# Even layer: input projections, sample-row scores and the index stage's loads put into one pipeline

## The chip, the cores and the metric

One NeuronCore of one Trainium2 chip runs the whole step; the metric is device time in microseconds (us). Before the change the median of three runs is 2185.47 us (2183.77 to 2185.55).

## The reference, cut to what matters

The model has two layers; the change touches the first part of layer 0 (the even layer). There are 1024 prompt rows and 8 sample rows (one new token for each of 8 sequences with 256 cached positions). All is float32.

```python
h = jnp.einsum('btd,de->bte', x, e_w_in[e])                  # 1024 + 8 rows, 1024 -> 4168 columns
q, k, v, qi, ki, wi, ga, ub, vb, gb = jnp.split(h, EVEN_SPLIT, axis=-1)
# index score of a key s for a row t, both groups; the 256 best keys are kept (64 for a sample row)
sc = jnp.einsum('bthd,bsd->bths', qi, ki) * (IDX_DIM ** -0.5)
score = jnp.einsum('bths,bth->bts', jax.nn.relu(sc), wi * (IDX_HEADS ** -0.5))
_, idx = lax.top_k(score, topk)
# attention logits: q.k / 8 - slope * distance, softmax over the kept keys; then times silu(ga)
```

q, k, v, qi, ga, ub, vb and gb are 512 columns wide each, ki is 64 and wi is 8.

## The kernel before

The program is a list of phases. Each has its own tiles and semaphores and ends in a barrier of all engines, after which the next phase issues its first load. The first three matter here.

**phase_even_in** (L105). SP loads an identity, x in row tiles of 128 (`x_tok`; the ninth tile is the 8 sample rows) and the weights of one column segment at a time into `w`, two deep. TensorE (PE) transposes x into `xT`, then runs `order`: for each segment (QI, Q, K, then KI with WI, 72 columns) nine groups, one for each row tile, of 8 accumulating matmuls (L186) into one of 8 PSUM banks. A float32 matmul shows in the trace as two instructions. VectorE (DVE) and ScalarE (ACT) take turns copying a bank to `stage` (L199), and POOL stores it to the scratch tensor `h` in DRAM (L156). The sample rows' group uses the same 512-column matmuls with 8 rows of output.

**phase_sample_scores** (L240). SP reads the sample rows of qi, wi, q and others back from `h`, two of them broadcast to all 128 partitions (L277 to L285, semaphore `own_in`), and the cached keys by page (L291, L292, `cache_in`). DVE forms the index scores (L336 to L343) and the logits (L345, L346) of the 8 sample rows. PE runs the GA segment beside it: `gate_columns` for row tiles 0 to 5, then a wait for DVE's scores and a transpose (L370), then tiles 6 and 7 and the sample rows, then the transposes of the logits (L377). The GA sample rows use `strips` (L95): four 128-column pieces of the weights go to four 32-row strips of the output. ACT makes the sigmoid and a copy, POOL multiplies them (L314), SP stores.

**phase_index** (L399). SP reads the identity, ki, qi and wi of all prompt rows back from `h` (L453 to L460, semaphore `in1`); PE waits for all eight loads, transposes ki and qi (L530), then runs 160 score matmuls (L537), each followed by a Relu on ACT and a weighted sum on DVE into `score`. Then SP's reload of q and k is transposed (L544), and PE runs the last four segments V, UB, VB, GB (L555, and L95 for the sample rows) out of `src`, loaded at L469 once the transposes are done. Meanwhile DVE searches each row's threshold, 31 rounds of seven counts (L633), and marks the kept keys (L659 to L663). The next phase, phase_attend, begins with a memset at L722.

Of the kernel before, what the change touches and what calls it, by code (L numbers as in the profile page):

```python
# [7 lines left out]
F32 = mybir.dt.float32  # L8
# [96 lines left out]
def phase_even_in(nc, g, xT):  # L105


    with ExitStack() as c:
        sb = lambda n, s, d=F32: c.enter_context(nc.sbuf_tensor(n, s, d))
        sem = phase_semaphores(nc, c, "")  # L110
        ident = sb("ei_ident", [P, P])
        x_tok = sb("ei_x", [P, NT + 1, D])
        w = sb("ei_w", [P, 2, KD, AW])
        w_small = sb("ei_ws", [P, KD, HD + H])
        stage = sb("ei_stage", [P, NB, AW])
        ps = [c.enter_context(nc.psum_tensor(f"ei_ps{i}", [P, AW], F32)) for i in range(NB)]
        ident_in, x_in = sem("ei_ident_in"), [sem(f"ei_x_in{t}") for t in range(NT + 1)]
        w_in = [sem(f"ei_w_in{i}") for i in range(2)]
        ws_in = sem("ei_ws_in")
        tr_done, xT_done = sem("ei_tr_done"), sem("ei_xT_done")  # L120
        mm_done = sem("ei_mm_done")
        ev_v, ev_a = sem("ei_ev_v"), sem("ei_ev_a")
        out_done = [sem(f"ei_out{i}") for i in range(NB)]
        W = g["e_w_in"]

        segs = [(COL_QI, AW), (COL_Q, AW), (COL_K, AW), (COL_KI, HD + H)]
        order = [(si, t) for si in range(len(segs)) for t in range(NT + 1)]
        wide = [si for si in range(len(segs)) if segs[si][1] == AW]
        h_d = g["h"]

        block = c.enter_context(nc.Block())

        @block.sync
        def _(sp):
            sp.dma_start(ident[:], g["c_ident"]).then_inc(ident_in, 16)
            for t in range(NT):
                sp.dma_start(x_tok[:, t, :], g["x_prompt"][t * P:(t + 1) * P, :]).then_inc(x_in[t], 16)
            sp.dma_start(x_tok[0:DB, NT, :], g["x_sample"]).then_inc(x_in[NT], 16)
            for n, si in enumerate(wide):
                if n >= 2:  # L140

                    sp.wait_ge(mm_done, (wide[n - 2] + 1) * (NT + 1))
                c0 = segs[si][0]
                sp.dma_start(w[:, n % 2], W[:, c0:c0 + AW].rearrange("(k p) n -> p k n", p=P)).then_inc(w_in[n % 2], 16)
                if n == 1:
                    sp.dma_start(w_small[:], W[:, COL_KI:COL_KI + HD + H].rearrange("(k p) n -> p k n", p=P)).then_inc(ws_in, 16)
            for b in range(NB):
                sp.wait_ge(out_done[b], 16 * len([n for n in range(len(order)) if n % NB == b]))

        @block.gpsimd  # L150
        def _(pool):

            for n, (si, t) in enumerate(order):
                c0, cw = segs[si]
                pool.wait_ge((ev_v, ev_a)[n % 2], n // 2 + 1)
                pool.dma_start(h_d[t * P:t * P + rows(t), c0:c0 + cw], stage[0:rows(t), n % NB, 0:cw]).then_inc(out_done[n % NB], 16)  # L156

        @block.tensor
        def _(pe):
            pe.wait_ge(ident_in, 16)  # L160
            for n in range(2 * (NT + 1)):

                t, half = n // 2, n % 2
                pe.wait_ge(x_in[t], 16)
                if n >= NB:
                    pe.wait_ge(xT_done, n - NB + 1)
                for j in range(4):
                    kd = half * 4 + j
                    m = rows(t)
                    last = nc.tensor.transpose(ps[n % NB][:, j * P:j * P + m], x_tok[0:m, t, kd * P:(kd + 1) * P], ident[0:m, 0:m])  # L170
                last.then_inc(tr_done, 1)
            pe.wait_ge(xT_done, 2 * (NT + 1))
            for n, (si, t) in enumerate(order):
                c0, cw = segs[si]
                if t == 0:
                    if cw == AW:
                        u = wide.index(si)
                        pe.wait_ge(w_in[u % 2], 16 * (u // 2 + 1))
                    else:
                        pe.wait_ge(ws_in, 16)  # L180
                if n >= NB:
                    m = n - NB
                    pe.wait_ge((ev_v, ev_a)[m % 2], m // 2 + 1)
                for kd in range(KD):
                    rhs = w[:, wide.index(si) % 2, kd, :] if cw == AW else w_small[:, kd, :]
                    last = nc.tensor.matmul(ps[n % NB][0:rows(t), 0:cw], xT[:, kd, t * P:t * P + rows(t)], rhs,  # L186
                                            start=(kd == 0), stop=(kd == KD - 1))
                last.then_inc(mm_done, 1)

        def evacuate(eng, copy, done, parity):  # L190
            for n, (si, t) in enumerate(order):
                if n % 2 != parity:
                    continue
                cw = segs[si][1]
                eng.wait_ge(mm_done, n + 1)
                if n >= NB:

                    eng.wait_ge(out_done[n % NB], 16 * (n // NB))
                copy(stage[0:rows(t), n % NB, 0:cw], ps[n % NB][0:rows(t), 0:cw]).then_inc(done, 1)  # L199

        @block.vector
        def _(dve):
            for n in range(2 * (NT + 1)):
                t, half = n // 2, n % 2
                dve.wait_ge(tr_done, n + 1)
                m = rows(t)
                nc.vector.tensor_copy(xT[:, half * 4:half * 4 + 4, t * P:t * P + m],
                                      ps[n % NB][:].rearrange("p (j n) -> p j n", j=4)[:, :, 0:m]).then_inc(xT_done, 1)
            evacuate(dve, nc.vector.tensor_copy, ev_v, 0)

        @block.scalar
        def _(act):
            evacuate(act, nc.scalar.copy, ev_a, 1)

# [21 lines left out]
def phase_sample_scores(nc, g, xT, score_s, lrow, room):  # L240
# [3 lines left out]
    with ExitStack() as c:  # L244
# [3 lines left out]
        ident = sb("sa_ident", [P, P])  # L248
        qb, qib = (r[:].rearrange("p c t -> p (c t)").rearrange("p (b n) -> p b n", b=DB) for r in room)
        w, stage, sig = sb("sa_w", [P, KD, AW]), sb("sa_stage", [P, 4, AW]), sb("sa_sig", [P, 2, AW])  # L250
        wib = sb("sa_wib", [P, DB, H])
        kc = sb("sa_kc", [P, DB, 2, AW])
        ic = sb("sa_ic", [P, DB, 2, HD])
        prod = sb("sa_prod", [P, 2, AW])
        lg = sb("sa_lg", [P, DB, 2, H])
        ix = sb("sa_ix", [P, DB, 2, H])
        sc = sb("sa_sc", [P, DB, 2])
        q_s, k_s, qi_s = sb("sa_q", [DB, AW]), sb("sa_k", [DB, AW]), sb("sa_qi", [DB, AW])
        ki_s, wi_s = sb("sa_ki", [DB, HD]), sb("sa_wi", [DB, H])
        lgn, ixn = sb("sa_lgn", [DB, H]), sb("sa_ixn", [DB, H])  # L260
        pt = sb("sa_pt", [1, 2 * DB], I32)
        ps = [c.enter_context(nc.psum_tensor(f"sa_ps{i}", [P, AW], F32)) for i in range(5)]
        ps_ga = [c.enter_context(nc.psum_tensor(f"sa_psga{i}", [P, AW], F32)) for i in range(3)]
        w_in, ga_mm, ga_read, sig_d, silu_d = (sem(f"sa_{n}") for n in ("w_in", "ga_mm", "ga_read", "sig_d", "silu_d"))
        ga_out = [sem(f"sa_ga_out{i}") for i in range(4)]
        copy_out = sem("sa_copy_out")
        own_in, cache_in, pt_in = sem("sa_own_in"), sem("sa_cache_in"), sem("sa_pt_in")
        link_v, scored, logits, tr_done, row_done = sem("sa_link"), sem("sa_scored"), sem("sa_logits"), sem("sa_tr"), sem("sa_rows")
        own_done, filled = sem("sa_own_done"), sem("sa_filled")
        block = c.enter_context(nc.Block())  # L270
        NOWN = 9

        @block.sync
        def _(sp):
            sp.dma_start(pt[:], g["page_table"]).then_inc(pt_in, 16)
            s = h_d[T:TA]
            sp.dma_start(qib, s[:, COL_QI:COL_QI + AW].partition_broadcast(P)).then_inc(own_in, 16)  # L277
            sp.dma_start(wib[:], s[:, COL_WI:COL_WI + H].partition_broadcast(P)).then_inc(own_in, 16)
            sp.dma_start(qb, s[:, COL_Q:COL_Q + AW].partition_broadcast(P)).then_inc(own_in, 16)
# [20 lines left out]
            for i in range(4):  # L300
                sp.wait_ge(ga_out[i], 16 * (len(range(i, NT, 4)) + (4 if i == NT % 4 else 0)))
# [2557 lines left out]
```

## Time and profile before

| | us |
|---|---|
| profiled execution, device time | 2195.87 |
| its span, first to last instruction | 2193.8 |
| median of three timed runs | 2185.47 |
| PE busy (share of the span) | 1832.5 (84%) |
| DVE busy | 1243.5 (57%) |
| ACT busy | 582.0 (27%) |
| POOL busy | 402.5 (18%) |

The phases run one after another, so a share of the whole span says little; each stretch has its own engine that ends last. The timeline by engine gives the start and length of merged runs of instructions and, in brackets, how long the engine was idle before and what released it. The windows view gives busy time and granted TensorE clock (1.00 is 2.4 GHz, 0.50 is 1.2 GHz) of a stretch.

### The profile page before, as it was taken

What the parts mean: (1) busy time and instruction counts of PE and PEld (TensorE: products, weight loads), DVE (VectorE), ACT (ScalarE), POOL (GpSimd) and SP (SyncE); (2) the same over time, 40 slices, a digit from 0 to 9 for tenths busy, and PEclk for the clock granted to TensorE, in tenths of its full rate; (3) what the DMA queues carried; (4) which work ended last, traced back from release to release, by engine and by line L of the source; (5) the groups of instructions that cost most, each with busy time, mean ns of one, the idle gap of its engine ahead of it and who ended that gap; (6) DMA issues with size and microseconds to landing.
All of it is one profiled execution on the core that took longest, in us unless ns stands there. A gap on an engine that the chain in (4) does not pass through costs nothing. (4 is left out here: it accounts for less than half of the span.)

```text
span 2193.8 us, 30598 instructions
## 1 busy us (share of the span) xinstructions
PE 1832.5 (84%) x11638; PEld 1061.9 (48%) x11638; DVE 1243.5 (57%) x2313; ACT 582.0 (27%) x1163; POOL 402.5 (18%) x376
## 2 busy tenths in 40 slices
PE   8999476899993899799747999977989977764977
PEld 4445234444442687447233666653454445653432
DVE  2000064888998765473467667677544244654287
ACT  0000004500012553121145555562121113432100
POOL 0001110000013554110000333320004222323030
PEclk9999688999996999797876999997989887987989
DMA  4200724212301100831175344434647275766401
GB/s 180 72 34 32 192 92 137 77 39 72 116 34 69 39 21 10 321 116 44 46 149 174 106 123 144 142 128 109 142 128 212 73 178 140 182 148 179 176 29 72
DMA packets 276431, 245.58 MB, mean 112 GB/s; under 512 B 131980, under 2 KB 229164, under 8 KB 276028
## 3 DMA queue, kind: packets, MB, share of 16 engines
q1 hardware_dynamic: 272276, 232.57, 36.0%
q0 software_dynamic: 2976, 9.02, 1.2%
q10 hardware_dynamic: 1040, 2.10, 0.4%
q8 instruction: 92, 1.51, 0.3%
q14 instruction: 47, 0.39, 0.1%
HBM read 161.53 MB, written 86.63 MB: 113 GB/s over the span
## 5 line engine op out<-in xcount | busy, mean ns | idle before, releaser
L1860 PE MATMUL ri_ps<-ri_xm,od_w 128*128 128x384 f32 (+1 forms) x768 | 233.0, 458 | 0.1
L555 PE MATMUL ix_ps<-ix_src,ei_xT 128*128 128x512 f32 x512 | 223.8, 599 | 9.4 <-DMA ix_src<-in_e_w_in 9.4
L1956 PE MATMUL ri_ps<-od_w,ri_xm 128*128 128x512 f32 x512 | 228.4, 609 | 0.0
L186 PE MATMUL ei_ps<-ei_w,ei_xT 128*128 128x512 f32 (+1 forms) x432 | 189.0, 600 | 4.0 <-DMA ei_w<-in_e_w_in 4.0
L1860 PEld LDWEIGHTS ri_ps<-ri_xm,od_w 128*128 128x128 f32 x768 | 145.1, 191 | 73.8 <-issue 2.3
L633 DVE TENSOR_SCALAR_CACHE_REDUCE ix_flags<-score,ix_cand 128x384 bf16<-128x384 f32 (+1 forms) x186 | 163.7, 942 | 12.2 <-DVE ix_cand L650 12.0
L555 PEld LDWEIGHTS ix_ps<-ix_src,ei_xT 128*128 128x128 f32 x512 | 98.0, 192 | 132.7 <-issue 123.0
L1956 PEld LDWEIGHTS ri_ps<-od_w,ri_xm 128*128 128x128 f32 x512 | 100.0, 196 | 125.5 <-issue 125.4
L1112 PE MATMUL go_psm<-go_w,go_srcT 128*128 128x512 f32 (+1 forms) x288 | 135.9, 632 | 4.5 <-DVE go_y L1254 4.2
L186 PEld LDWEIGHTS ei_ps<-ei_w,ei_xT 128*128 128x128 f32 (+1 forms) x432 | 77.8, 181 | 114.4 <-issue 114.4
L199 DVE COPY ei_stage<-ei_ps 128x512 f32<-128x512 f32 (+2 forms) x18 | 10.6, 588 | 196.5 <-PE ei_ps L186 196.5
L770 PE MATMUL at_pss<-at_kz,qT 128*128 128x512 f32 (+3 forms) x192 | 79.9, 528 | 31.5 <-POOL at_kz L722 31.5
L730 POOL TENSOR_TENSOR at_bias<-at_alibi,score 128x128 f32<-128x128 f32 (+7 forms) x64 | 91.9, 1436 | 74.9 <-ACT at_alibi L791 74.3
L1112 PEld LDWEIGHTS go_psm<-go_w,go_srcT 128*128 128x128 f32 (+1 forms) x288 | 54.9, 194 | 79.0 <-issue 76.8
L2413 PE MATMUL wk_i<-od_big 64*64 64x128 f32 (+1 forms) x1024 | 70.2, 353 | 20.6 <-DVE wk_ak L2588 8.4
L361 PE MATMUL sa_psga<-sa_w,ei_xT 128*128 128x512 f32 x128 | 60.3, 635 | 30.7 <-DMA sa_w<-in_e_w_in 30.7
L1382 PE MATMUL co_psm<-od_w,co_srcT 128*128 128x512 f32 (+1 forms) x144 | 68.4, 631 | 17.1 <-DVE co_y L1436 16.9
L840 DVE CUSTOM_DVE_ANT_0 at_s<-at_pss,at_bias 128x128 f32<-128x128 f32 (+7 forms) x64 | 48.4, 756 | 49.1 <-PE at_pss L770 48.8
L2171 DVE SCALAR_TENSOR_TENSOR ri_xm<-ri_xT,ri_mu,ri_xm 128x384 f32<-128x384 f32 (+1 forms) x144 | 70.9, 567 | 6.2 <-ACT ri_xm L1973 5.8
L760 PE MATMUL at_pso<-at_v,at_pT 128*128 128x64 f32 x576 | 73.3, 274 | 0.0
L2269 DVE TENSOR_TENSOR ri_xT<-ri_xT,ri_ps 128x512 f32<-128x512 f32 (+1 forms) x18 | 11.6, 642 | 108.1 <-ACT ri_xT L2089 108.0
L760 PEld LDWEIGHTS at_pso<-at_v,at_pT 128*128 128x128 f32 x576 | 71.9, 197 | 0.3 <-issue 0.2
(329 smaller groups left out, 3010.6 us busy)
## 6 DMA issues: line engine op xcount, KB each, us to landing
ix_src<-in_e_w_in SPq DMA_DIRECT2D x4, 2048.0 KB, 11.1
scratch_h<-ix_stage SPq DMA_DIRECT2D x32, 256.0 KB
od_w<-in_c_w_in SPq DMA_DIRECT2D x16, 512.0 KB, 5.7
od_w<-in_c_w_in SPq DMA_DIRECT2D x4, 2048.0 KB, 8.8
ei_w<-in_e_w_in SPq DMA_DIRECT2D x3, 2048.0 KB, 19.3
scratch_h<-ei_stage POOLq DMA_DIRECT2D x24, 256.0 KB, 2.3
ix_src<-scratch_h SPq DMA_DIRECT2D x3, 2048.0 KB, 9.2
go_uvg<-scratch_h SPq DMA_DIRECT2D x8, 768.0 KB, 10.5
```

The costliest lines, as they stand in the source:

```text
L186: last = nc.tensor.matmul(ps[n % NB][0:rows(t), 0:cw], xT[:, kd, t * P:t * P + rows(t)], rhs, start=(kd == 0), stop=(kd == KD - 1))
L555: last = nc.tensor.matmul(ps[n % NB][:], xT[:, kd, t * P:(t + 1) * P], w_rest[s % 2][:, kd], start=(kd == 0), stop=(kd == KD - 1))
L633: link(nc.vector.tensor_scalar(flags[:, at:at + x.shape[1]], x, s, 0.0, op, ALU.add, accum_out=cnt[:, j:j + 1]), wait=j == NTOP - 1)
L730: nc.gpsimd.tensor_tensor(bias[:, u % 2, 0:n], alibi[:, u % 2, 0:n], score[:, OFF[i]:OFF[i] + n], ALU.add).then_inc(bias_d, 1)
L760: last = nc.tensor.matmul(ps_o[i % 2][:, h * HD:(h + 1) * HD], pT[:, n % 4, j * P:(j + 1) * P], v[:, k0 + j, h * HD:(h + 1) * HD], start=( ...
L770: last = nc.tensor.matmul(ps_s[u % 2][:, s0:s0 + w], qT[:, h // 2, i * P:(i + 1) * P], kz[:, h, s0:s0 + w], start=True, stop=True)
L1112: last = nc.tensor.matmul(ps_m[k][0:m, cs], srcT[:, k, kd, 0:m], w[:, kd, cs], start=(kd == 0), stop=(kd == KD - 1))
L1382: last = nc.tensor.matmul(ps_m[k][0:m, hf * AW:(hf + 1) * AW], srcT[:, k, kd, 0:m], wo[hf][:, kd], start=(kd == 0), stop=(kd == KD - 1))
L1860: last = nc.tensor.matmul(out[:, 0:wd], w[:, ct % 2, kd, i * P:(i + 1) * P], xm[:, i, kd, lo:lo + wd], start=(kd == 0), stop=(kd == KD - 1))
L1956: last = nc.tensor.matmul(out[:], xm[:, j, kd, t * P:(t + 1) * P], w[:, a, kd], start=(kd == 0), stop=(kd == KD - 1))
L2171: nc.vector.scalar_tensor_tensor(xm[:, n % 2, kd, lo:lo + m], xT[:, kd, lo:lo + m], mu[:, MIX[n], kd:kd + 1], xm[:, n % 2, kd, lo:lo + m], ...
L2413: return nc.tensor.matmul(out, lhsT, rhs, start=start, stop=stop, skip_group_check=True)
```

## The change

phase_even_in and phase_sample_scores become one phase. Its segments are QI, KI, Q, K, GA. The sample rows of every 512-column segment use `strips`. DVE's score work for the sample rows is cut into one step for each group of Q and K. GA is gated on DVE from PSUM (ACT makes the sigmoid) and stored by POOL. At its end the phase reads qi into `w[:, 0]` and ki into a part of `x_tok`, from `h`; the identity, `w`, `x_tok` and `xT` stay allocated through phase_index, which therefore issues neither these loads nor a wait for them on PE. phase_index loads the weights of V and UB at its start into `x_tok`, and those of VB and GB into `w` after the q and k transposes; its `stage` and `sig` lie over `qiT`.

```diff
+        segs = [(COL_QI, AW), (COL_KI, HD + H), (COL_Q, AW), (COL_K, AW), (COL_GA, AW)]
+        who = ["v" if n % 2 == 0 or order[n][0] == GA else "a" for n in range(len(order))]
...
+            load_w(0)
+            sp.dma_start(w_small[:], W[:, COL_KI:COL_KI + HD + H]...).then_inc(ws_in, 16)
+            sp.dma_start(pt[:], g["page_table"]).then_inc(pt_in, 16)
+            load_w(1)
+            sp.wait_ge(pt_in, 16)
+            sp.wait_ge(tr_done, 2 * (NT + 1))
...                                    # 16 pages of ic and of kc (kc lies over x_tok)
+            load_w(2)                  # waits for QI's last matmul
+            stored_rows(small_rows[QI])
+            sp.dma_start(qib, ...partition_broadcast(P)).then_inc(index_in, 16)
+            sp.dma_start(qi_s[:], ...).then_inc(index_in, 16)
+            stored_rows(small_rows[KI])
...                                    # wib, ki_s, wi_s: index_in
+            load_w(3)                  # waits for Q's last matmul
+            stored_rows(small_rows[Q])
+            sp.dma_start(qb, ...partition_broadcast(P)).then_inc(q_in, 16)
...                                    # q_s: q_in; after K's rows are stored k_s: k_in
+            sp.wait_ge(mm_done, first[K] + NT + 1)
+            for n in range(first[QI], first[KI] + NT):
+                stored_rows(n)
+            sp.dma_start(w[:, 0], tok(COL_QI, AW)).then_inc(next_in, 16)
+            for o in range(2):
+                sp.dma_start(kid[:, :, o * HD:(o + 1) * HD], tok(COL_KI, HD)).then_inc(next_in, 16)
+            sp.wait_ge(next_in, 48)
...                                    # POOL, in its store loop:
+                if n == first[GA] + 3:
...                                    # waits for the KI and K stores, then p_k, p_idx_k, s_k, s_idx_k
...                                    # PE, in its group loop:
+                if stripped(n):
+                    last = strips(nc, ps[n % NB], lambda kd: xT[:, kd, TA - STRIP:TA], lambda kd: w[:, wide.index(si) % 2, kd])
...                                    # PE after the loop: wait scored, 2 transposes; wait logits, 16 transposes
...                                    # DVE, in its loop over the groups, after the copy of group n:
+                    if si == GA:
+                        k = n - first[GA]
+                        dve.wait_ge(sig_d, k + 1)
+                        nc.vector.tensor_tensor(stage[0:m, n % NB, 0:wd], sig[0:m, k % 2, 0:wd], src, ALU.mult).then_inc(ev["v"], 1)
...
+                if n == first[Q] + 2:
+                    own_score()        # waits index_in, ic_in
+                if first[Q] + 2 <= n < first[Q] + 2 + DB:
+                    index_score(n - first[Q] - 2)
+                if n == first[K] + 1:
+                    index_sum()
+                if first[K] + 2 <= n < first[K] + 2 + DB:
+                    logit(n - first[K] - 2)    # the first waits q_in, kc_in
+            own_logit()                # waits k_in
...                                    # phase_index
-            sp.dma_start(ident[:], g["c_ident"]).then_inc(in1, 16)
-            sp.dma_start(kid[:, :, 0:HD], tok(COL_KI, HD)).then_inc(in1, 16)
-            sp.dma_start(kid[:, :, HD:P], tok(COL_KI, HD)).then_inc(in1, 16)
-            sp.dma_start(src[0][:], tok(COL_QI, AW)).then_inc(in1, 16)
...                                    # wi, upper, bits_f, bits_i as before, then k
+            load_w(0)
+            load_w(1)
             sp.wait_ge(pe_done, n1)
+            sp.dma_start(src[0], tok(COL_Q, AW)).then_inc(in2, 16)
             sp.wait_ge(pe_done, n3)
+            load_w(2)
+            load_w(3)
...                                    # POOL
+            pool.wait_ge(pe_done, 2)
+            nc.gpsimd.memset(ones, 1.0).then_inc(ones_done, 1)
...                                    # PE
-            pe.wait_ge(in1, 16 * 8)
...                                    # DVE
-            dve.wait_ge(in1, 16 * 8)
+            dve.wait_ge(in1, 16 * 4)
```

## Rows read from the trace of the kernel before

**Rows 1.** Windows: stretch, length, busy (count) by engine, clock, DMA share, GB/s.

```profile
20.70:225.30 204.60, 204.50 (x576) 93.07 (x576) 10.59 (x18) 8.54 (x18) 19.19 (x35) 0.99 0.14 51
339.50:351.40 11.90, 0.00 (x0) 0.00 (x0) 0.00 (x0) 0.00 (x0) 2.85 (x3) 0.52 0.88 253
351.40:418.00 66.60, 65.74 (x214) 37.84 (x215) 48.46 (x81) 47.36 (x94) 0.00 (x0) 0.96 0.18 63
664.00:687.10 23.10, 0.15 (x8) 0.00 (x0) 22.35 (x22) 0.43 (x2) 1.79 (x2) 0.58 0.03 12
```

**Rows 2.** Timeline of PE to 420 us: start, length, instructions, idle before and releaser.

```profile
20.68 188.99 PE L186 MATMUL ei_ps<-ei_w,ei_xT 128*128 128x512 f32 x432 [3.98 <-DMA ei_w<-in_e_w_in]
209.59 15.61 PE L186 MATMUL ei_ps<-ei_ws,ei_xT 128*128 128x72 f32 x144
255.92 44.25 PE L361 MATMUL sa_psga<-sa_w,ei_xT 128*128 128x512 f32 x96 [30.72 <-DMA sa_w<-in_e_w_in]
314.88 0.59 PE L370 MATMUL sa_ps<-sa_ident,sa_sc 128*8 128x128 f32 x2 [14.71 <-DVE sa_sc L343]
334.77 1.91 PE L377 MATMUL sa_ps<-sa_ident,sa_lg 128*8 128x128 f32 x16 [1.57 <-DVE sa_lg L346]
351.43 7.35 PE L530 MATMUL ix_ps<-ix_ident,ix_src 128*128 128x128 f32 x40 [14.75 <-DMA ix_bits_i<-c_bits_i]
```

**Rows 3.** Timeline of PE from 420 us, the rest segments.

```profile
433.06 58.16 PE L555 MATMUL ix_ps<-ix_src,ei_xT 128*128 128x512 f32 x128 [9.44 <-DMA ix_src<-in_e_w_in]
...
493.04 55.20 PE L555 MATMUL ix_ps<-ix_src,ei_xT 128*128 128x512 f32 x128
548.17 1.95 PE L95 MATMUL ix_ps<-ix_src,ei_xT 128*32 128x128 f32 x64
550.05 55.20 PE L555 MATMUL ix_ps<-ix_src,ei_xT 128*128 128x512 f32 x128
```

**Rows 4.** Groups by line and shape, 20 to 226 us: busy, mean ns, idle before.

```profile
L186 PE MATMUL ei_ps<-ei_w,ei_xT 128*8 128x512 f32 x48 | 21.1, 592 | 0.0
```

**Rows 5.** Timeline of DVE: sample-row work, then phase_index.

```profile
269.23 0.68 DVE L323 TENSOR_TENSOR sa_q<-sa_q,sa_k 8x512 f32<-8x512 f32 x1 [44.86 <-DMA sa_ident<-c_ident]
...
293.72 1.22 DVE L339 TENSOR_REDUCE sa_ix<-sa_prod 128x16 f32<-128x1024 f32 x1
294.97 2.29 DVE L336 TENSOR_TENSOR sa_prod<-sa_ic,kT 128x1024 f32<-128x1024 f32 x1
...
361.16 0.42 DVE L610 TENSOR_SCALAR score<-ix_rel,ix_wi 128x384 f32<-128x384 f32 x1 [9.56 <-ACT ix_rel L578]
...
418.10 0.23 DVE L623 TENSOR_SCALAR score<-ix_upper 128x128 f32<-128x128 f32 x1
```

**Rows 6.** Timeline of POOL: the last stores of phase_even_in and what follows.

```profile
225.74 0.52 POOL L156 DMA_DIRECT2D scratch_h<-ei_stage  x1 [0.53 <-ACT ei_stage L199]
230.11 0.47 POOL L305 MEMSET score_s<- 128x449 f32 x1 [3.85 <-POOLq L76]
...
294.92 1.26 POOL L314 TENSOR_TENSOR sa_stage<-sa_stage,sa_sig 128x512 f32<-128x512 f32 x1 [5.96 <-ACT sa_stage L392]
...
688.09 7.50 POOL L722 MEMSET at_kz<- 64x4096 f32 x2 [22.30 <-POOLq L76]
```

**Rows 7.** Timeline of SP's queue: the read-back, and phase_index's first load.

```profile
230.41 0.37 SPq L277 DMA_DIRECT2D kT<-scratch_h  x1
...
231.45 23.23 SPq L279 DMA_DIRECT2D qT<-scratch_h  x1
...
339.52 0.37 SPq L453 DMA_DIRECT2D ix_ident<-c_ident  x1
```

**Rows 8.** Window 13 us after the copy of v to its output is issued.

```profile
565.00:570.00 5.00, 5.00 (x13) 2.19 (x12) 4.25 (x12) 0.00 (x0) 0.00 (x0) 1.00 0.21 82
```

**Rows 9.** Timeline of ACT at the end of phase_sample_scores.

```profile
333.26 0.28 ACT L389 ACTIVATE sa_sig<-sa_psga 128x128 f32<-128x128 f32 x1 [0.84 <-PE sa_psga L95]
...
336.72 2.02 ACT L395 ACTIVATE lrow<-sa_ps 8x512 f32<-8x512 f32 x4 [3.02 <-PE sa_ps L377]
```

More of the change, by code:

```diff
@@ L102, in strip_rows @@
     return slice((j + 1) * STRIP - DB, (j + 1) * STRIP)
[L105 to L213, printed above, removed]
@@ L244, in phase_sample_scores, with index_rows, phase_index @@
+def index_rows(x_tok):
+    return x_tok[:].rearrange("p t d -> p (t d)")[:, 2 * DB * AW:2 * DB * AW + T].rearrange("p (t n) -> p t n", t=NT)
+def phase_index(nc, g, xT, qT, kT, score, score_s, ident, w, x_tok):
     with ExitStack() as c:
@@ L257, in phase_sample_scores @@
[L257 to L264, printed above, removed]
@@ L352, in _ @@
-        @block.tensor
-        def _(pe):
-            def gate_columns(t):
-                if t >= 3:
-                    pe.wait_ge(ga_read, t - 2)
-                if t == NT:
-                    last = strips(nc, ps_ga[t % 3], lambda kd: xT[:, kd, TA - STRIP:TA], lambda kd: w[:, kd])
-                else:
-                    for kd in range(KD):
-                        last = nc.tensor.matmul(ps_ga[t % 3][:], xT[:, kd, t * P:(t + 1) * P], w[:, kd], start=(kd == 0), stop=(kd == KD - 1))
-                last.then_inc(ga_mm, 1)
-            pe.wait_ge(w_in, 16)
-            for t in range(NT - 2):
-                gate_columns(t)
-            pe.wait_ge(own_in, 16 * NOWN)
-            pe.wait_ge(scored, 1)
-            for pg in range(2):
-                last = nc.tensor.transpose(ps[4][0:DB, pg * P:(pg + 1) * P], sc[:, :, pg], ident[:])
-            last.then_inc(tr_done, 1)
-            for t in range(NT - 2, NT + 1):
-                gate_columns(t)
-            pe.wait_ge(logits, DB)
-            for h in range(H):
-                for pg in range(2):
-                    last = nc.tensor.transpose(ps[h // 2][0:DB, (h % 2) * PAST + pg * P:(h % 2) * PAST + (pg + 1) * P],
-                                               lg[:, :, pg, h], ident[:])
-            last.then_inc(tr_done, 1)
@@ L381, in _ @@
-        @block.scalar
-        def _(act):
-            act.dma_start(w[:], g["e_w_in"][:, COL_GA:COL_GA + AW].rearrange("(k p) n -> p k n", p=P)).then_inc(w_in, 16)
-            for t in range(NT + 1):
-                m = AW if t < NT else P
-                act.wait_ge(ga_mm, t + 1)
-                if t >= 2:
-                    act.wait_ge(silu_d, t - 1)
-                nc.scalar.activation(sig[:, t % 2, 0:m], ps_ga[t % 3][:, 0:m], ACT.Sigmoid).then_inc(sig_d, 1)
-                if t >= 4:
-                    act.wait_ge(ga_out[t % 4], 16 * (t // 4))
-                nc.scalar.copy(stage[:, t % 4, 0:m], ps_ga[t % 3][:, 0:m]).then_inc(ga_read, 1)
-            act.wait_ge(tr_done, 2)
-            for q in range(4):
-                last = nc.scalar.activation(lrow[:, 2 * q:2 * q + 2, 0:PAST],
-                                            ps[q][0:DB, :].rearrange("p (h s) -> p h s", h=2), ACT.Copy, scale=HD ** -0.5)
-            last.then_inc(row_done, 1)
@@ L400, in phase_index @@
-def phase_index(nc, g, xT, qT, kT, score, score_s):
-    with ExitStack() as c:
-        sb = lambda n, s, d=F32: c.enter_context(nc.sbuf_tensor(n, s, d))
-        sem = phase_semaphores(nc, c, "")
-        h_d = g["h"]
-        ident = sb("ix_ident", [P, P])
         wi = sb("ix_wi", [P, NT, H])
-        src = [sb(f"ix_src{i}", [P, NT, AW]) for i in range(2)]
-        kid = src[1][:, :, 0:P]
+        src, kid = [w[:, i] for i in range(2)], index_rows(x_tok)
         qiT = sb("ix_qiT", [P, 4, T])
@@ L444, in phase_index @@
         gates = [n for n, (s, t) in enumerate(rest) if is_gate[s]]
-        w_rest = src
-        w_in, rest_out = [sem(f"ix_w_in{i}") for i in range(2)], [sem(f"ix_rest_out{i}") for i in range(4)]
+        over = x_tok[:].rearrange("p t d -> p (t d)")
+        w_rest = [over[:, s * KD * AW:(s + 1) * KD * AW].rearrange("p (k n) -> p k n", k=KD) for s in range(2)] + src
+        w_in, rest_out = [sem(f"ix_w_in{i}") for i in range(4)], [sem(f"ix_rest_out{i}") for i in range(4)]
         zeroed = sem("ix_zeroed")
@@ L548, in _ @@
                 if t == 0:
[L549 removed]
+                    pe.wait_ge(w_in[s], 16)
                 bank_free()
                 if t == NT:
[L552 removed]
+                    last = strips(nc, ps[n % NB], lambda kd: xT[:, kd, TA - STRIP:TA], lambda kd: w_rest[s][:, kd])
                 else:
                     for kd in range(KD):
[L555 removed]
+                        last = nc.tensor.matmul(ps[n % NB][:], xT[:, kd, t * P:(t + 1) * P], w_rest[s][:, kd],
                                                 start=(kd == 0), stop=(kd == KD - 1))
@@ L2790, in even_layer @@
             score, qT, kT = (c2.enter_context(nc.sbuf_tensor(n, s, F32)) for n, s in (("score", [P, OFF[NT]]), ("qT", [P, 4, T]), ("kT", [P, 4, T])))
-            with nc.sbuf_tensor("ei_xT", [P, KD, TA], F32) as xT:
-                phase_even_in(nc, g, xT)
-                phase_sample_scores(nc, g, xT, score_s, lrow, (qT, kT))
-                phase_index(nc, g, xT, qT, kT, score, score_s)
+            with ExitStack() as c3:
+                xT, ident, w, x_tok = (c3.enter_context(nc.sbuf_tensor(f"ev_{n}", s, F32)) for n, s in (
+                    ("xT", [P, KD, TA]), ("ident", [P, P]), ("w", [P, 2, KD, AW]), ("x", [P, NT + 1, D])))
+                phase_even_in(nc, g, xT, score_s, lrow, (qT, kT), ident, w, x_tok)
+                phase_index(nc, g, xT, qT, kT, score, score_s, ident, w, x_tok)
             phase_attend(nc, g, qT, kT, score)
```

319 lines of the change are left out of this document (215 added, 104 removed).

## The prediction, made before the changed kernel ran

> **What bounds the kernel now.** The phases run one after another, so I read the windows first: which engine works in each stretch, and where none does [rows 1]. From 20.7 to 225.3 us PE is busy 204.5 of 204.6 us at clock 0.99: the projections are bound by PE. Behind it come stretches in which PE hardly runs; from 339.5 to 351.4 nothing runs but DMA (0.88 of its engines) and memsets of POOL. Then the timeline of PE says what ended each of PE's holes [rows 2]: the GA weights' load (30.72 us of idle time), DVE's `sa_sc` (14.71), a small wait for `sa_lg` (1.57), and the eight loads of phase_index (14.75). From 351.4 to 418.0 PE is the bound again (65.74 of 66.6). Last, DVE's timeline shows what ends phase_index [rows 5]: the threshold search starts at 418.10 with the masks, and DVE is busy 22.35 us of the last 23.1 [rows 1], up to 1 us before the next phase starts at 688.09 [rows 6]. PE's last segment ends near 664, since after it PE is busy 0.15 us of 23.1 [rows 1]. So whatever the change does to PE after 418 is not on the path; what counts is how early DVE's search starts, and that is set by PE's transposes of qi and ki at 351.43 plus 66.7 us of PE-bound work (418.10 - 351.43). The sum has to find the new time of that one instruction.
>
> **The change part by part: the joined phase.** PE starts its first matmul at 20.68 in both. The loads ahead of it (identity, x, first weights) are the same, in the same order; the second weights move behind the small ones, and 32 page loads come in only after x is transposed, all behind the first weights on SP's queue. Bounds: 4.0 us earlier (the idle time before that matmul [rows 2]) to as much later if the page loads share the engines with it; I take 0, since they are issued behind it.
>
> *QI, Q, K.* They take 209.59 - 20.68 = 188.9 us [rows 2]. The three sample-row groups are 48 of the 432 instructions [rows 4]. A segment at full clock has 128 in 55.20 us [rows 3], 0.431 each, so they cost 20.7. A group by `strips` costs 1.88 us from its start to the next segment (550.05 - 548.17), three of them 5.6. Saved: 15.1; left: 173.8.
>
> *KI* is moved, not changed: 15.6 us. *GA* costs one segment with strips as in phase_index: 550.05 - 493.04 = 57.0 us [rows 3]. It needs no wait inside if the evacuation keeps up: for each group of 6.9 us ACT makes one sigmoid (at most four times the 0.28 of 128 columns [rows 9]) and DVE one multiply out of PSUM. The latter is not in this trace; its bounds are half and all of the 1.22 us that a 128x1024 operation takes [rows 5], both far below 6.9.
>
> So PE's stream ends at 20.7 + 173.8 + 15.6 + 57.0 = 267.1 us.
>
> *DVE's work for the sample rows* is hidden beneath that stream: 32 operations of 1.22 us [rows 5] are 39 us in 116 us of Q and K. What it could cost is a wait in DVE's queue, with PSUM copies behind it. It waits at two places. At Q's third group it needs the rows of QI and KI, stored, read back and broadcast. Before, such a read-back took from 230.41 [rows 7] to 269.23 [rows 5], 38.8 us, beside a 2 MB weight load and a 2 MB copy. QI ends at 78.6 and KI at 94.2, so by that figure the last lands near 135, where DVE arrives at 115. The first bank that DVE then owes is Q's fifth group, which PE needs again eight groups on, in K's fourth, near 173. At K's second group it needs q: issued near 153, landed near 192, DVE there from 166; PE needs the bank near 224 (GA's third group). The bounds are 0 and what runs past 38 and 32 us of margin; I take 0. SP's queue is in order too: the third weights go out at 78.6 for a need at 152, the fourth at 152 for 210.
>
> *The end of the phase.* After PE's last strip: 0.59 + 1.91 us of transposes [rows 2] and ACT's last quarter of 2.02 us [rows 9], all within 3.5. The stores are later: sigmoid 0.28 [rows 9], multiply, then four stores of POOL at about 0.5, where before there was one copy and one store. Before, PE ended at 225.2 (209.59 + 15.61), the last store was issued at 225.74, and the next phase began at 230.11 [rows 6]: 4.9 us. I add 0.45 for sigmoid and multiply in place of a 0.2 us copy and 1.6 for three more stores: 7.0. The lower end is 3.5 plus the 0.8 between ACT's end (338.74 [rows 9]) and the next issue at 339.52 [rows 7]: 4.3; the upper is 7.0 plus the 4.9 us seen here once more, 12. Of the three transfers that must be done by then, the reload of qi starts after K (210.0), and p_k's copy near 238; of the same 2 MB copy of v, issued at 552.39, little is left 13 us later (DMA share 0.21 [rows 8]), so 267 covers both.
>
> The row that speaks against this end: a DVE operation on two SBUF operands started 0.05 us after a POOL operation (294.97 against 294.92) and took 2.29 in place of 1.22 [rows 5, 6]; the two engines can hold each other up. DVE now works beside all of POOL's stores, but those are eight slots of 6.9 us deep, so only the four last ones, which share their time with own_logit (operations of 0.68 us and less [rows 5]), could be late; by the rows I take 0 and keep 2 us.
> SBUF — State Buffer of the Trainium skill ("SBUF: two separate sides", the box on DVE blocking DMA) states the other side of it: POOL cannot write its DMA descriptors while DVE holds the shared port. By that rule the end comes 1 to 2 us later and the time is near 2110; no run here shows a POOL store so delayed.
>
> So phase_index begins at 267.1 + 7.0 = 274.1.
>
> **Phase_index.** PE waits for nothing and starts its transposes at 274.1, in place of 351.43: **77.3 us earlier**. Their 7.35 us stay; they follow an idle gap in both and ACT's copies pace them. DVE still waits for wi and three constants. Its first unit is due 9.7 us after PE's start (361.16 - 351.43); before, eight loads with 2 MB among them took 11.9 us, now four small ones go first. So 0, at most 2.2, and DVE has 18 us of slack in the 66.6 [rows 1]. K, V's and UB's weights (6 MB) load under the score matmuls, most of the 66.6 us. The 9.44 us wait at 433.06 [rows 3] goes, worth nothing: PE ends 23 us before DVE as it is. From DVE's search on all stays.
>
> **Sum.** 2195.87 - 77.3 = 2118.6 for a profiled execution. That of before lies 10.4 us over the median of the timed runs; the same distance gives 2185.47 - 77.3 = 2108.2. I say 2108.
>
> **The rivals.**
> *The reload is not hidden, so the rows are not "kept" but only read earlier* (they do go through `h`). For it: the old wait was 11.9 us [rows 1], and the end of the phase waits for the reload, the p_k copy and the stores. Against: 57 us of GA to hide in. Price: up to 11.9, so 2120; with a tail of 12 in place of 7 instead, 2113.
> *PE stalls in the stream.* DVE's wait for q or for the index rows outlasts its margin by 20 to 50 us, as when the store, the queue behind 2 MB of weights and the 38.8 us add up; 2128 to 2158. For it: SP's queue once took 23.23 us over one issue [rows 7]; against: the margins of 38 and 32 us on top of a read-back as slow as the worst one seen.
> *Other side: DVE's wait for q holds PE longer than the old holes did.* Place: logit(0), in front of all of DVE's copies. It costs nothing until q lands 71 us after its issue (224 - 153), then one for one; from 148 us on the kernel is slower (71 + 77), and at 200 us it would be 2237. Only a read-back four times as slow as any in the trace does this.
> *More gain.* The first weights come up to 4 us sooner, and the two POOL collisions on DVE go: 2102.
>
> **How the numbers follow.** Forecast, 2102 to 2116: 0.68. Unhidden reload or longer tail, 2116 to 2126: 0.14. Stall in the stream, 2126 to 2180: 0.08. Other side: 0.04. More gain, below 2102: 0.06. The range of 8 in 10 is 2099 to 2126: the bounds of tail (minus 2.7, plus 5), reload (plus 11.9), start (4 either way). About 0.2% (4.4 us) is what a measurement of this kernel can tell from no change; every case but two lies far outside it: faster 0.95, same 0.01, slower 0.04.
>
> **What would show it.** In the trace after: PE without a hole over 2 us from 20.7 to near 267; strip groups near 1.9 us with three of them new; phase_index's transposes near 274; the masks near 341 and phase_attend near 611. I am wrong in mechanism if PE waits inside the joined phase, if the time from PE's last strip to phase_index is over 12 us, or if DVE's first unit waits for a load. I am wrong in the premise if the search, from masks to last mark, is not the 269 us it is now.

## The result, and the profile after

The changed kernel took 2119.39 us (median of 4 runs) against 2185.51 us for the kernel before: ratio 0.9687, 95% interval [0.966, 0.9714], faster by 62 to 74 us. Timed once more in the last group of experiments it took 2112.77 us against 2186.36 us: 0.9668 [0.9654, 0.9682]. The forecast was 2108 in a range of 2099 to 2126, with 0.95 on faster. The profiled execution took 2120.29 us (span 2118.5) where 2118.6 had been worked out, but that closeness is luck: 5.4 us of the gain were lost ahead of phase_attend, and in this execution the stages behind it happened to be 3.4 us shorter (1505.7 us before, 1502.3 after), a way that varies by 10 us (see below).

The timeline of PE in the changed kernel, from the first weights to the first score matmuls (start, length, instructions, idle time before and its releaser); it answers to [rows 2]:

```profile
20.32 58.13 PE L282 MATMUL ei_ps<-ev_w,ev_xT 128*128 128x512 f32 x128 [3.96 <-DMA ev_w<-in_e_w_in]
78.38 1.96 PE L95 MATMUL ei_ps<-ev_w,ev_xT 128*32 128x128 f32 x64
80.27 15.61 PE L282 MATMUL ei_ps<-ei_ws,ev_xT 128*128 128x72 f32 x144
95.81 55.20 PE L282 MATMUL ei_ps<-ev_w,ev_xT 128*128 128x512 f32 x128
150.94 1.96 PE L95 MATMUL ei_ps<-ev_w,ev_xT 128*32 128x128 f32 x64
152.82 55.20 PE L282 MATMUL ei_ps<-ev_w,ev_xT 128*128 128x512 f32 x128
207.95 1.96 PE L95 MATMUL ei_ps<-ev_w,ev_xT 128*32 128x128 f32 x64
209.83 55.20 PE L282 MATMUL ei_ps<-ev_w,ev_xT 128*128 128x512 f32 x128
264.96 1.95 PE L95 MATMUL ei_ps<-ev_w,ev_xT 128*32 128x128 f32 x64
266.85 0.39 PE L288 MATMUL ei_ps<-ev_ident,ei_sc 128*8 128x128 f32 x2
267.07 1.91 PE L296 MATMUL ei_ps<-ev_ident,ei_lg 128*8 128x128 f32 x16
276.03 1.94 PE L526 MATMUL ix_ps<-ev_ident,ev_x 128*128 128x128 f32 x8 [7.05 <-PEq L76]
```

No row between 20.32 and 266.85 carries a wait: the four segments, KI and the four strip groups (1.96 us each) run without a hole. The only idle time left is 7.05 us at the change of phase. The same in windows, by stage (stretch, length, busy and count by engine, granted clock, DMA share, GB/s), to set beside [rows 1]:

```profile
20.32:266.85 246.53, 246.53 (x912) 120.09 (x913) 56.57 (x68) 14.43 (x27) 30.65 (x57) 0.99 0.39 117
266.85:276.03 9.18, 2.13 (x23) 1.52 (x19) 2.13 (x5) 2.29 (x5) 2.53 (x6) 0.78 0.09 30
276.03:342.10 66.07, 64.42 (x215) 36.52 (x216) 48.54 (x82) 47.20 (x94) 2.81 (x3) 0.98 0.38 133
342.10:616.17 274.07, 233.39 (x819) 108.96 (x817) 244.62 (x602) 30.88 (x60) 10.61 (x10) 0.93 0.16 54
```

The cuts are the end of PE's last strip, PE's first transpose of phase_index, DVE's first mask and POOL's first instruction of phase_attend. In the kernel before the last three were at 351.43, 418.10 and 688.09 [rows 2, 5, 6]: the change is ahead by 75.40, 76.00 and 71.92 us. So 4.08 us are lost again inside the search, which it was not meant to touch. Of the 75.40, 15.4 are gained by the end of the projections (225.2, 209.83) and 60.0 in the stretch from there to the transposes: 126.2 us before, now GA's 57.02 and an end of 9.18.

What DVE did for the sample rows, at the two places where it was forecast to wait, then its first unit of phase_index and its first mask (timeline of DVE, changed kernel):

```profile
116.71 0.69 DVE L379 COPY ei_stage<-ei_ps 128x512 f32<-128x512 f32 x1 [13.04 <-PE ei_ps L282]
117.32 0.67 DVE L326 TENSOR_TENSOR ei_qi_s<-ei_qi_s,ei_ki_s 8x512 f32<-8x512 f32 x1
...
174.67 1.22 DVE L351 TENSOR_TENSOR ei_prod<-ev_x,qT 128x1024 f32<-128x1024 f32 x1 [6.06 <-DMA ei_q_s<-scratch_h]
...
285.16 0.42 DVE L607 TENSOR_SCALAR score<-ix_rel,ix_wi 128x384 f32<-128x384 f32 x1 [4.10 <-ACT ix_rel L575]
...
342.10 0.23 DVE L620 TENSOR_SCALAR score<-ix_upper 128x128 f32<-128x128 f32 x1
```

The index rows were there already. For q, DVE waited 6.06 us, 13.9 us after the issue at 160.73, and PE never noticed. The first unit of phase_index waited for ACT, not for a load. So none of the three signs of a wrong mechanism appeared: no wait of PE inside the joined phase, no end of over 12 us, no unit held by a load. The sign of a wrong premise did: from masks to the last mark it is 273.04 us in place of 268.99.

### The profile page after: what moved, and what is told of

The parts are those of the page before. It is cut to its first block and busy times, and to the rows that moved or that the text cites. A ratio compares the mean times of both kernels' runs of the same rounds, so it can differ in the third digit from the quotient of the medians.

```text
span 2118.5 us, 30882 instructions
## 1 busy us (share of the span) xinstructions
PE 1809.3 (85%) x11782; PEld 1061.2 (50%) x11782; DVE 1244.2 (59%) x2322; ACT 577.0 (27%) x1154; POOL 399.7 (19%) x388
## 5 line engine op out<-in xcount | busy, mean ns | idle before, releaser
L282 PE MATMUL ei_ps<-ev_w,ev_xT 128*128 128x512 f32 x512 | 223.7, 599 | 4.0 <-DMA ev_w<-in_e_w_in 4.0
L282 PEld LDWEIGHTS ei_ps<-ev_w,ev_xT 128*128 128x128 f32 x512 | 98.0, 192 | 127.0 <-issue 126.8
L552 PE MATMUL ix_ps<-ev_w,ev_xT 128*128 128x512 f32 x256 | 110.4, 593 | 0.0
L552 PE MATMUL ix_ps<-ev_x,ev_xT 128*128 128x512 f32 x256 | 110.3, 593 | 0.0
L552 PEld LDWEIGHTS ix_ps<-ev_w,ev_xT 128*128 128x128 f32 x256 | 48.5, 190 | 60.7 <-issue 60.7
L552 PEld LDWEIGHTS ix_ps<-ev_x,ev_xT 128*128 128x128 f32 x256 | 48.5, 190 | 60.5 <-issue 60.5
```

What stands on the lines that cost most here:

```text
L552: last = nc.tensor.matmul(ps[n % NB][:], xT[:, kd, t * P:(t + 1) * P], w_rest[s][:, kd], start=(kd == 0), stop=(kd == KD - 1))
```

## The experiments

All are the changed kernel with one edit, unless said otherwise. Where a stage is compared, the times come from the traces. Five kernels (GA's weights late, q's read-back late, DVE's work behind the loop, the own logit moved, 28 memsets) were executed once, so for these only the cuts of that one trace are used; the others have five or six timed runs. In the kernels whose edit leaves PE's stream alone, its last strip ends between 265.56 and 267.39 us, so a cut is good to about 1 us.

**The parts of the change.** First the strips, undone in the changed kernel (QI, Q and K) and then put alone into the kernel before:

```
-stripped = lambda n: order[n][1] == NT and order[n][0] != KI
+stripped = lambda n: order[n][1] == NT and order[n][0] == GA
```

> The changed kernel with the sample rows of QI, Q and K as three ordinary groups of full-width matmuls; only GA keeps strips. Theory, PE-bound stream: each group goes from 1.9 to 6.9 us, so the masks come 15 us later (357 in place of 342) and the time rises 15 us. Rival, the stream is paced by loads or by DVE's waits as well: the masks come later by less than 10 us.

Masks at 356.90, 14.80 later; 2128.97 us, ratio 0.9724 [0.9696, 0.9752] to the kernel before.

```
 in phase_even_in of the kernel before:
+if stripped(n):
+    last = strips(nc, ps[n % NB], lambda kd: xT[:, kd, TA - STRIP:TA], lambda kd: w[:, wide.index(si) % 2, kd])
...
+for j in range(4):
+    pool.dma_start(h_d[T:TA, c0 + j * P:c0 + (j + 1) * P], stage[strip_rows(j), n % NB, 0:P])
```

> The kernel before with one part of the change alone: the sample rows of QI, Q and K computed by strips, everything else as before. Theory, the parts add up: three groups fall from 6.9 to 1.9 us, the masks come 15 us earlier than in the kernel before (403 in place of 418.1) and the time falls 15 us, which with the 60 us of removed holes makes the whole change. Rival, the strips' gain is taken back behind them, by four stores each or by a longer wait for the next weights: the masks come less than 8 us earlier.

Masks at 403.09, 15.01 earlier; 2170.98 us, ratio 0.9921 [0.9905, 0.9938]. Both directions come within 0.3 us of the forecast 15.1: in this stretch, which PE bounds, PE's instructions are the price, and nothing ahead of the masks takes it back. Next the reload:

```
 phase_even_in:  -the loads of w[:, 0] (qi) and kid (twice), and the wait for them
 phase_index:    +the same three loads first on SP's queue, counted by in1
-dve.wait_ge(in1, 16 * 4)
+dve.wait_ge(in1, 16 * 7)
+pe.wait_ge(in1, 16 * 7)
```

> The changed kernel with the index rows and keys (qi, ki) loaded at the start of phase_index again, as before, and not under the GA segment. Theory, hidden reload: the 2 MB load and the two small ones stand in front of PE's first transposes, as in the kernel before (11.9 us from the first issue), so masks come 8 to 12 us later (350 to 354) and the time rises as much. Rival, the reload holds the joined phase's end and is paid there anyway: phase_index starts sooner by several us without it, and the masks come less than 4 us later.

The first loads of phase_index were issued at 275.50, 9.14 us after the last strip: just as long as with the reload, which thus held nothing up at that end. PE (timeline of that run) stood for them:

```profile
286.90 1.97 PE L526 MATMUL ix_ps<-ev_ident,ev_x 128*128 128x128 f32 x8 [18.41 <-DMA ix_bits_i<-c_bits_i]
```

Masks at 352.99, 10.89 later; 2127.4 us, 0.9711 [0.9682, 0.9741]. The rival of an unhidden reload is out. Then GA's weights, issued as late as in the kernel before:

```
-load_w(3)                      (behind KI's read-backs)
+sp.wait_ge(mm_done, first[K] + NT + 1)
+load_w(3)
```

> The changed kernel with GA's 2 MB of weights loaded only when K's last matmul is done (209.8), as in the kernel before, where PE then stood for 30.72 us. Theory, crowded queue: a 2 MB load takes 9 us by itself, and the 30.72 us came from the stores, read-backs and the 2 MB copy beside it; the hole before GA is 9 to 13 us and the masks come as much later (351 to 355). Rival, the load is slow by itself at this place: a hole of 20 us or more.

Timeline of PE in that run, and windows over the hole and what follows it:

```profile
218.62 57.15 PE L283 MATMUL ei_ps<-ev_w,ev_xT 128*128 128x512 f32 x128 [9.39 <-DMA ev_w<-in_e_w_in]
```
```profile
200.00:209.00 9.00, 9.00 (x82) 4.62 (x80) 1.56 (x2) 0.58 (x1) 1.08 (x2) 1.00 0.08 29
...
218.62:221.00 2.38, 2.38 (x3) 1.18 (x4) 0.00 (x0) 0.00 (x0) 0.00 (x0) 0.50 0.86 231
221.00:223.00 2.00, 2.00 (x4) 0.85 (x3) 0.00 (x0) 0.00 (x0) 0.00 (x0) 0.61 1.04 388
223.00:226.00 3.00, 3.00 (x8) 1.33 (x8) 0.00 (x0) 0.00 (x0) 0.00 (x0) 1.00 1.13 351
```

The bare load costs a hole of 9.39 us where the old one was 30.72 [rows 2]; 4.9 of the rest was the old phase end (225.2 to 230.11, [rows 6]), the remaining 16 us the queue ahead of it and the traffic beside it, which this run does not part. The hole costs more than itself: behind it the granted clock is 0.50 (1.2 GHz) and 0.61 before it is 1.00 again, and the segment takes 57.15 us in place of 55.20. Masks at 352.83, 10.73 later.

**DVE's queue, the mechanism of the rival on the other side.**

```
 stored_rows(small_rows[Q])
+sp.wait_ge(mm_done, first[GA] + 2)
 sp.dma_start(qb, ...)
```

> The changed kernel with q's read-back issued only after GA's second group (near 224 in place of 160.7). Theory, DVE's queue holds PE: a read-back takes some 14 us, so q lands near 237, logit(0) waits for it with DVE's copies of K behind it, PE's bank for GA's third group comes free 3 us later; PE has a hole of 13 to 17 us before GA's third group, and masks and time come as much later, one for one (masks 355 to 359). Rival, there is slack elsewhere (the eight banks, DVE's idle time): a hole of under 6 us.

Timelines of PE and DVE in that run:

```profile
209.69 14.00 PE L283 MATMUL ei_ps<-ev_w,ev_xT 128*128 128x512 f32 x32
239.71 43.58 PE L283 MATMUL ei_ps<-ev_w,ev_xT 128*128 128x512 f32 x96 [16.02 <-DVE ei_stage L380]
```
```profile
236.45 1.23 DVE L352 TENSOR_TENSOR ei_prod<-ev_x,qT 128x1024 f32<-128x1024 f32 x1 [67.98 <-DMA ei_q_s<-scratch_h]
237.71 1.22 DVE L353 TENSOR_REDUCE ei_lg<-ei_prod 128x16 f32<-128x1024 f32 x1
238.96 0.69 DVE L380 COPY ei_stage<-ei_ps 128x512 f32<-128x512 f32 x1
```

PE stops before GA's third group, as forecast, until DVE has got past its wait, one multiply, one reduction and the late copy of K. DVE waited 68 us to cost PE 16: the banks absorb some 50 of them. That it goes one for one from there is read from this chain; no second delay was run. Masks at 360.38, 18.28 later and 1.4 beyond the forecast range, which had only the hole: behind it come 2.2 us of slower matmuls (43.58 in place of 41.4, three quarters of 55.20), the first 3.3 us at a granted clock of 0.50.

```
-own_score, index_score, index_sum, logit placed between DVE's copies of Q and K
+the same calls, in the same order, after the loop over the groups
```

> The changed kernel with DVE's work for the sample rows behind the last group of GA and not between the groups. Theory, it was hidden: 39 us for the 32 operations of 1.22 us, and some 4 us of small ones, come on top; phase_index starts near 316 to 320 and the masks near 382 to 386. Rival, DVE and POOL had held each other up when they ran side by side, and the stream or the tail gets shorter by some us without it: phase_index starts before 312.

Phase_index at 316.99, masks at 383.05: 40.95 us later. That is what the hiding was worth; no collision with POOL gives any of it back (the 32 operations take 1.22 us each in both places). Between ACT's last operation (ended 315.99) and SP's first issue of phase_index (316.96) lay 0.97 us: what a change of phase costs when all stores have long landed.

**The end of the joined phase.** Two edits: the last four strip stores on SP, and the own logit taken away from beside them.

```
 POOL:  +if n == N - 1: continue
 SP:    +sp.wait_ge(ev[who[N - 1]], done[N - 1])
        +for j in range(4): sp.dma_start(h_d[T:TA, COL_GA + j * P:...], stage[strip_rows(j), (N - 1) % NB, 0:P])
        +...                           (and a wait until the four have landed)
```

> The changed kernel with the last four strip stores issued by SP instead of POOL. Theory, POOL's stores: the 9.1 us from PE's last strip to phase_index (7.0 predicted) are set by POOL's four issues (2.02 us) and by how late POOL is through with them, so phase_index starts 1 to 2.5 us sooner (273.5 to 275 in place of 276.0), the time falls as much. Rival, closing: what takes the time comes after the stores have landed (barriers, giving back the phase's semaphores), and phase_index starts within 0.4 us of 276.0.

```
+if n == first[GA] + 4: own_logit()
 ...
-own_logit()                    (behind the loop over the groups)
```

> The changed kernel with the own logit (three DVE operations, 1.5 us) moved from the end of the phase to behind GA's fifth group, so that DVE is free while POOL issues the last four stores (267.97 to 269.99). Theory, shared port: POOL's last stores come late because DVE holds the port that POOL needs to write them out; without DVE's three operations phase_index starts 1 to 2 us sooner (274 to 275 in place of 276.0). Rival, POOL's own queue: four stores of POOL take that long by themselves, and phase_index starts within 0.4 us of 276.0.

POOL's timeline in the changed kernel, POOL's with the own logit moved, and SP's with the stores on SP:

```profile
267.97 2.02 POOL L238 DMA_DIRECT2D scratch_h<-ei_stage  x4 [0.65 <-DVE ei_stage L377]
275.99 1.95 POOL L496 MEMSET ix_kiT<- 64x1024 f32 x2 [6.00 <-POOLq L76]
```
```profile
267.04 2.03 POOL L238 DMA_DIRECT2D scratch_h<-ei_stage  x4 [0.65 <-DVE ei_stage L377]
275.07 1.95 POOL L497 MEMSET ix_kiT<- 64x1024 f32 x2 [6.00 <-POOLq L76]
```
```profile
268.30 1.36 SPq L229 DMA_DIRECT2D scratch_h<-ei_stage  x4
273.55 0.39 SPq L460 DMA_DIRECT2D ix_wi<-scratch_h  x1
```

From the end of PE's last strip to phase_index's first transpose it is 9.18 us in the changed kernel, 9.19 with the own logit moved (that run was 0.9 us ahead already before, so its absolute times mislead), and 6.19 with the stores on SP. So the stores set it, and not DVE's work beside them. Behind POOL's last issue lie 6.0 us, behind SP's 3.9, as behind POOL's single last store of the kernel before (3.85, [rows 6]). Why four on POOL take 2.1 us longer to be done is not settled; nor is why the same four are done in 5.3 in the kernel with ordinary groups for QI, Q and K. SBUF — State Buffer of the Trainium skill ("SBUF: two separate sides") states that POOL cannot write its descriptors while DVE runs an operation in a two-port mode. No view tells the mode of the three DVE operations here, so the rule is not tested; a delay by them is not seen, since POOL's four issues take 2.02 us beside them and 2.03 without. With SP the time was 2113.79 us, 0.9655 [0.9626, 0.9684], an interval that overlaps the changed kernel's, so the cuts show this gain and the time alone does not; the masks came 1.78 us earlier.

**The search.** The rounds of its loop were 7.29 us in the changed kernel and 7.14 before, with the same instructions; the time is lost ahead of each round's first count. The loop's place in DVE's instruction stream had changed (by 11 in my count of the program, which no view shows), so it was moved:

```
+pad = sb("pad", [P, 64])
+for i in range(53):            (28 in the second run)
+    nc.vector.memset(pad[:, i:i + 1], 0.0)
...
 for n in range(2 * (NT + 1)):  (DVE's first loop)
```

> The changed kernel with 53 one-column memsets more at the head of the vector engine's work, where it is idle until 6.46 us. They only move the threshold search's loop 53 places on in DVE's instruction stream. Theory, place: the 0.15 us that each of the 30 rounds lost (7.14 us before, 7.29 after) comes from where the loop lies in the stream; before and after the loop's start differs by 11 places, and 53 more makes 64, so the rounds return to 7.14 us, masks still at 342.1, search 269 in place of 273, phase_attend at 612, time about 4 us below the changed kernel. Rival, state: the rounds are slower for another reason (what the joined phase leaves behind, or traffic), they stay at 7.29 us and the time is that of the changed kernel.

> The changed kernel with 28 one-column memsets at the head of DVE's work (53 in the run before brought the search's rounds from 7.29 to 7.14 us). Theory, coarse: what counts is whether the 28 places of the loop lie across a border of blocks of 64 places or more; then 28 places on it is clear of it and the rounds are 7.14 us. Rival, fine: blocks of 32 or 16 places; the loop, which begins 7 places from the good one modulo either, lies badly again, with rounds of 7.2 to 7.3 us.

The first counts of two rounds, timeline of DVE: the kernel before, the changed one, and that with 28 memsets.

```profile
433.26 0.61 DVE L633 TENSOR_SCALAR_CACHE_REDUCE ix_flags<-score,ix_cand 128x384 bf16<-128x384 f32 x1 [0.42 <-DVE ix_cand L650]
...
440.41 0.61 DVE L633 TENSOR_SCALAR_CACHE_REDUCE ix_flags<-score,ix_cand 128x384 bf16<-128x384 f32 x1 [0.41 <-DVE ix_cand L650]
```
```profile
357.42 0.61 DVE L630 TENSOR_SCALAR_CACHE_REDUCE ix_flags<-score,ix_cand 128x384 bf16<-128x384 f32 x1 [0.57 <-DVE ix_cand L647]
...
364.73 0.61 DVE L630 TENSOR_SCALAR_CACHE_REDUCE ix_flags<-score,ix_cand 128x384 bf16<-128x384 f32 x1 [0.57 <-DVE ix_cand L647]
```
```profile
357.72 0.61 DVE L633 TENSOR_SCALAR_CACHE_REDUCE ix_flags<-score,ix_cand 128x384 bf16<-128x384 f32 x1 [0.42 <-DVE ix_cand L650]
...
364.87 0.61 DVE L633 TENSOR_SCALAR_CACHE_REDUCE ix_flags<-score,ix_cand 128x384 bf16<-128x384 f32 x1 [0.41 <-DVE ix_cand L650]
```

The idle time of 0.57 us falls to 0.42 and 0.41, the round to 7.15; with 53 memsets it is 7.14. From masks to phase_attend it is 274.07 us in the changed kernel, 268.29 with 53, 268.32 with 28. Of these 5.8 us the loop's place is 4.3: 0.147 in each of the 29 steps from one round to the next. The rest is chance of another kind. The changed kernel's last interval of the loop is 8.01 us against 6.96, and the round behind the loop 7.13 against 6.33, since there POOL's gate multiplies meet DVE's smallest operations (POOL and DVE in the changed kernel, then the first two of these DVE operations with 28 memsets):

```profile
567.99 1.27 POOL L504 TENSOR_TENSOR ix_qiT<-ix_qiT 128x512 f32<-128x512 f32 x1 [5.60 <-ACT ix_qiT L592]
574.86 1.73 POOL L504 TENSOR_TENSOR ix_qiT<-ix_qiT 128x512 f32<-128x512 f32 x2 [5.60 <-ACT ix_qiT L592]
```
```profile
568.07 1.21 DVE L647 TENSOR_TENSOR ix_cand<-ix_v,ix_bits_i 128x7 int32<-128x7 int32 x1 [0.16 <-DVE ix_v L643]
575.43 0.71 DVE L642 SCALAR_TENSOR_TENSOR ix_flip<-ix_cnt,ix_bits_f 128x7 int32<-128x7 f32 x1
576.18 0.42 DVE L643 TENSOR_TENSOR ix_v<-ix_v,ix_flip 128x7 int32<-128x7 int32 x1
```
```profile
564.62 0.17 DVE L650 TENSOR_TENSOR ix_cand<-ix_v,ix_bits_i 128x7 int32<-128x7 int32 x1 [0.16 <-DVE ix_v L646]
570.94 0.17 DVE L645 SCALAR_TENSOR_TENSOR ix_flip<-ix_cnt,ix_bits_f 128x7 int32<-128x7 f32 x1
```

Operations of 0.17 us take 0.42 to 1.21 beside a multiply: 1.8 us in all. With the faster rounds all but one of POOL's multiplies fall beside the counts, which keep their time (1.14 and 1.27 us either way), and only one small operation is hit, for 0.24 us with 28 memsets and 0.36 with 53.

With 53 the median was 2108.87 us, 0.9632 [0.9602, 0.9661]. The rounds answered to both moves, so the place is the cause as far as these runs go (the tile `pad`, too, is new in both), and that 28 places do as well as 53 speaks for coarse blocks. The DMA view shows fetches of instructions: of the changed kernel's window 352 to 358 us (the first round), and of the 28-memset kernel's 342 to 349 us, ahead of its loop, the row of the instruction queue q14 (packets, MB, share) is

```profile
q14 instruction: 1, 0.01, 0.4%
```
```profile
q14 instruction: 1, 0.01, 0.4%
```

With 28 memsets the first round has no such row; q14 is the queue whose packet has moved with them. So in the changed kernel a block comes in while the loop's first round runs. It is not fetched again each round (6 instruction packets between 358 and 566 us, as in the other). Runtime: NRT & Kernel Launch of the Trainium skill ("Instruction fetch mechanics") says that code comes in by blocks, and that a taken branch out of the window held forces a fetch; no fetch per round is seen here, only 0.15 us. What those 0.15 us are, and whether that packet is DVE's, is open.

**Both findings together, and the changed kernel once more.**

> The changed kernel with both things that the runs found: 28 one-column memsets at the head of DVE's work (search loop 28 places on) and the last four strip stores issued by SP. Theory, they add: phase_attend 5.3 us sooner by the loop and 1.8 us by the stores, near 609 in place of 616.2, and the time 7 us below the changed kernel's, near 2112. Rival, the earlier start is lost again in phase_index, whose first units wait for the same loads: phase_attend not before 610.5.

> The changed kernel once more. It has two uses: the time that the other runs of this call stand against, and a second profile. Theory, the first profile is typical up to phase_attend and the stages after it vary from run to run: masks at 342.1 and phase_attend at 616.2 within 0.6 us again, while the way from phase_attend to the end (1502.3 us) differs by 2 us or more. Rival, that way repeats within 1 us, and the 4 to 5 us by which its last third was shorter than in the kernel before belong to the change.

POOL's timeline, first instruction of phase_attend, changed kernel again and with both:

```profile
616.35 7.50 POOL L719 MEMSET at_kz<- 64x4096 f32 x2 [39.58 <-POOLq L76]
```
```profile
605.67 7.50 POOL L728 MEMSET at_kz<- 64x4096 f32 x2 [33.83 <-POOLq L76]
```

With both: 2106.26 us, 0.9625 [0.9606, 0.9643], clear of the changed kernel's 0.9668 [0.9654, 0.9682] in the same group. Of the 10.68 us at phase_attend (7 were forecast), 5.75 come from the search (274.07 to 268.32) and 2.99 from the tail (9.18 to 6.19), so they add; the other 1.9 come from the stream (1.5) and the way to the masks (0.5), which the edits leave alone: the variation of a cut. The changed kernel repeats to 0.2 us up to phase_attend (masks 342.28), but from there to the end it took 1492.2 us (2108.5 - 616.35) where the first profile had 1502.3. So the stages behind vary by 10 us between two executions of one kernel.

## Why the prediction came out as it did

*Right, by its steps.* Start 20.32 (20.68); QI, Q and K 173.97 without KI (173.8); KI 15.54 (15.6); GA 57.02 (57.0): the stream ended at 266.85 where 267.1 was forecast. DVE's work cost nothing in place, and 41 us out of it. The reload was hidden, and is worth 10.9. DVE's wait for q did have its margin, and the bank it would have cost is the one named, GA's third group.

*The tail was mis-sized*: 7.0 forecast, 9.18 measured, inside the bounds of 4.3 to 12. The step at fault is "four stores of POOL at about 0.5": the issues were right (2.02 us), but I charged nothing for the 2.1 us by which four of them are done later than one.

*"From DVE's search on all stays" failed.* The premise of 269 us to the last mark came out as 273.04 (to phase_attend 269.99 and 274.07). The loop's place, which nothing in the working looked at, cost 4.25. The collisions with POOL did not go, as the rival of more gain had it; they moved. In the kernel before they hit two operations of the marks, which took 1.57 and 1.98 us (0.75 and 0.88 alone); without such hits the marks are 2.0 us shorter:

```profile
657.61 1.57 DVE L661 SCALAR_TENSOR_TENSOR ix_flags<-ix_flags,ix_rem 128x512 f32<-128x512 f32 x1
663.50 1.98 DVE L662 SCALAR_TENSOR_TENSOR score<-score,ix_v,ix_flags 128x640 f32<-128x640 f32 x1
```

In the changed kernel they hit the end of the search for 1.8. So 4.25 less 0.2 is the whole loss.

*The sum at phase_attend*: 77.3 forecast, 71.92 measured. Tail 2.18, search 4.08, less 0.25 for the stream and 0.60 for the stretch to the masks (66.07 for 66.67): 5.4, the whole difference. (The range is not quite what its bounds add up to: 2101 and 2129 for 2099 and 2126.)

*The step from profile to median* took off 10.4 us because the profile before lay that far above its runs. The profile after lay 0.9 above its own: the offset belongs to one execution, not to the kernel, since the stages after phase_attend vary by as much. So the profile's 2118.6 was met only by luck. The forecast of the median is not touched by it, since 2118.6 - 10.4 is the same as 2185.47 less the gain. With the measured 71.9 that gives 2113.6, between the two medians of 2119.39 and 2112.77. Of the 11.2 us by which the first median missed 2108.2, 5.4 are the sum's; the other 5.8 do not show in the second median and stay open.

## What to carry to other kernels

In a stretch that one engine bounds, count that engine's instructions and price the rest by how late it may come: the stream came out at 246.5 us where 246.4 was summed. Look for the loss where the change did not touch: compare every stage's length, not only the end, and suspect a loop whose code has moved, or small operations that now run beside another engine's large ones. Before a loss is put down to a cause, look at the single operations that became longer. A gain of this size is read better from stage cuts (0.2 us apart in two profiles of one kernel, up to 1.8 between kernels alike in that stretch) than from one profile's total (10 us apart).

## What the hardware showed that was not expected

A loop on DVE ran 0.15 us a round slower (7.29, 7.14) in the kernel in which a packet of instructions came in during its first round; 28 or 53 memsets ahead of it, in idle time, cured that. POOL's multiply of 1.27 us stretched DVE's operations on seven columns from 0.17 to as much as 1.21 us, while DVE's counts beside such multiplies kept their 1.14 and 1.27. Four last stores on POOL hold the phase's end 2.1 us longer behind the last issue than four on SP (6.0, 3.9). A hole of 9 to 16 us in PE costs 2 to 3 us more behind it, at a granted clock of 0.50; [rows 3] had shown it already (58.16 behind a wait of 9.44, 55.20 without), and QI's segment shows it behind one of 3.96 (58.13).
